# Layer norm sums on token quarters inside the convolution, a first weight transfer of its own, dummy matmuls moved, and waits by bank

## The reference, cut to what matters

```python
def conformer_conv_mixer(h, w_pw1, b_pw1, w_dw, b_dw, ln_g, ln_b, w_pw2, b_pw2):
    u = h @ w_pw1 + b_pw1
    a, gate = jnp.split(u, 2, axis=-1)
    u = a * jax.nn.sigmoid(gate)
    z = lax.conv_general_dilated(u, w_dw[:, None, :], (1,), [(CONV_WIDTH - 1, 0)], ...) + b_dw
    mu = jnp.mean(zf, axis=-1, keepdims=True)
    var = jnp.mean(jnp.square(zf - mu), axis=-1, keepdims=True)
    zf = (zf - mu) * lax.rsqrt(var + NORM_EPS) * ln_g + ln_b
    return jax.nn.silu(zf) @ w_pw2 + b_pw2
for i in range(DEPTH):
    x = x + mixer_i(rmsnorm(x, norm_mix_g[i]))          # 0: retention, 1: conformer_conv_mixer
    x = x + hierarchical_moe(rmsnorm(x, norm_ffn_g[i]))
return rmsnorm(x, final_norm_g)
```

## Time and profile before

| | |
|---|---|
| median of 3 runs | 1625.94 us (1623.56 to 1627.71) |
| profiled execution, its own time | 1625.24 us |
| its span | 1623.4 us |
| PE, DVE, ACT, POOL busy | 92%, 61%, 27%, 26% |
| mean granted clock of PE | 0.978 |
| retention and start | 0 to 441 us |
| router and experts, layer 0 | 441 to 918 us |
| norm, products, convolution | 918 to 1059 us |
| layer norm, last products | 1059 to 1129 us |
| router and experts, layer 1, final norm | 1129 to 1623 us |

### The profile page before, as it was taken

How to read it: one execution, slowest core, us unless ns; L and a number is a source line. 1 busy time by engine, 2 the same in 40 slices (tenths; PEclk the granted TensorE clock), 3 DMA queues, 4 the chain that set the end, 5 groups by cost and what they waited for, 6 DMA issues and landing times.

```text
span 1623.4 us, 45311 instructions
## 1 busy us (share of the span) xinstructions
PE 1495.5 (92%) x18938; PEld 982.5 (61%) x18939; DVE 989.1 (61%) x1662; ACT 446.2 (27%) x731; POOL 423.7 (26%) x371
## 2 busy tenths in 40 slices
PE   7999999999989999998789899979999988889996
PEld 5868778688645555554445588747555555445553
DVE  4222022220378888776566889952788877668877
ACT  5242422322432222221112422154222212112222
POOL 3434334244101212121111255523021211112121
PEclk9999999999999999999999999999999999999998
DMA  9212212122299999999999620116399999999996
GB/s 377 85 64 71 93 53 104 52 104 104 87 377 428 429 428 428 429 428 428 429 429 426 277 100 20 41 57 266 118 417 430 428 429 429 428 428 430 428 428 271
DMA packets 33849, 457.60 MB, mean 282 GB/s; under 512 B 3840, under 2 KB 3968, under 8 KB 6400
## 3 DMA queue, kind: packets, MB, share of 16 engines
q1 hardware_dynamic: 33648, 456.57, 67.4%
q10 hardware_dynamic: 144, 0.18, 0.0%
HBM read 454.64 MB, written 2.10 MB: 281 GB/s over the span
## 4 chain that ended last, share of the span: by engine, by line
PE 66%; DMA 21%; DVE 10%; issue 1%; ACT 1%; SPq 0%; POOL 0%; DVEq 0%; ACTq 0%
PE ps L803 15%; PE ps L697 9%; PE ps L699 9%; PE ps L698 9%; DMA area_b<-w_gu 9%; PE ps L820 8%; PE ps L739 7%; PE ps L786 5%; DMA ring<-w_down 5%; DMA ring<-w_gu 4%; DVE area_c L1321 4%; DMA hT<-w_down 3%; PE ps L888 2%; DVE ring L1321 2%; PE ps L880 1%
## 5 line engine op out<-in xcount | busy, mean ns | idle before, releaser
L1159 DVE TENSOR_TENSOR x<-x,ps 128x1024 f32<-128x1024 f32 x384 | 450.9, 1216 | 90.7 <-PE ps L786 90.7
L456 POOL TENSOR_SCALAR slot_tok<-trig,slot_now 128x512 fp32r<-128x512 f32 x94 | 147.0, 1563 | 710.7 <-PE ps L786 710.7
L425 POOL TENSOR_TENSOR w_lo<-ring,w_hi 128x512 fp32r<-128x512 f32 x176 | 236.8, 1348 | 359.4 <-ACT w_hi L475 359.2
L803 PE MATMUL ps<-ring,hgT 128*32 128x256 f32 x4160 | 259.5, 391 | 48.4 <-DMA ring<-w_gu 28.6
L803 PEld LDWEIGHTS ps<-ring,hgT 128*32 128x32 f32 x4160 | 131.1, 111 | 145.0 <-issue 41.1
L475 ACT CAST w_hi<-ring 128x512 fp32r<-128x512 f32 x176 | 108.9, 623 | 346.8 <-PE ps L699 346.3
L739 PE MATMUL ps<-area_a,block_rows 128*32 128x256 f32 x3072 | 187.7, 386 | 0.6 <-DVE block_rows L1120 0.6
L549 ACT ACTIVATE y_hi<-ps,slots 128x256 fp32r<-128x256 f32 x94 | 44.5, 474 | 396.7 <-PE ps L820 396.7
L739 PEld LDWEIGHTS ps<-area_a,block_rows 128*32 128x32 f32 x3072 | 102.3, 113 | 72.1 <-issue 9.5
L820 PE MATMUL ps<-ring,aT_e 128*32 128x256 f32 x2080 | 125.7, 382 | 3.6 <-DMA ring<-w_down 3.6
L697 PE MATMUL ps<-w_hi,hT_hi 128*128 128x512 f32 x320 | 125.0, 391 | 2.9 <-DVE hT_lo L1351 2.9
(11 more groups left out here) (216 smaller groups left out, 1941.5 us busy)
## 6 DMA issues: line engine op xcount, KB each, us to landing
ring<-w_gu SPq DMA_DIRECT2D x88, 2048.0 KB, 28.1
ring<-w_down SPq DMA_DIRECT2D x44, 2048.0 KB, 29.0
area_c<-w_gu SPq DMA_DIRECT2D x20, 2048.0 KB, 29.3
area_b<-w_gu SPq DMA_DIRECT2D x20, 2048.0 KB, 31.8
hT<-w_down SPq DMA_DIRECT2D x20, 2048.0 KB, 32.4
ring<-w_pw SPq DMA_DIRECT2D x6, 2048.0 KB, 10.8
ring<-w_qk SPq DMA_DIRECT2D x4, 2048.0 KB, 8.4
ring<-w_v SPq DMA_DIRECT2D x4, 2048.0 KB, 8.7
```

Of the source, the lines that this page charges most:

```text
L425: nc.gpsimd.tensor_tensor(w_lo[:, place, :], ring[:, s, at:at + 512], w_hi[:, place, :].bitcast(F32), ALU.subtract).then_inc(lo_ready, 1)
L456: nc.gpsimd.tensor_scalar(slot_tok[:, :], tok_number, slot_now[:, 0:1], None, ALU.is_equal).then_inc(tok_hot[l], 1)
L803: last = nc.tensor.matmul(ps[32 * g:32 * g + 32, 2, 0:256], hgT[:, n * (KT // 2) + k, :], gate_up[n][:, k, :, g * P:(g + 1) * P], start=(n ...
L1159: return V.tensor_tensor(x[:, i, :].rearrange("p (g c) -> p g c", g=4), x[:, i, :].rearrange("p (g c) -> p g c", g=4), ps[:, bank:bank + 4 ...
```

## The change

- **Start.** The first two weight tiles come in a DMA of their own (0.5 MB). ACT loads a table before it waits, and casts the first tiles between the norm tiles. PE runs three dummies, and `x_added` rises by 4 after half of `norm_lo`.
- **Waits by bank.** In the first product and the first product of the convolution, PE waits at bank m for `hT_lo` of tile m, no longer for four tiles at once. The two dummies and waits ahead of the latter are gone.
- **Experts.** `know_rows` for the next block stands at the head of a block instead of at the end of the one before; that after the last block is gone. Two dummies stand between the last two puts, and one instead of two after `combined` reaches 2. ACT casts only two tiles ahead of the norm.
- **Layer norm.** POOL's sum is gone. Inside the taps of m = 1, PE sums tiles 0 to 3 (`sum_channels`, four 32-column groups), and minus that sum by 512 is added as `shift` to all 8 tiles: by DVE to tiles 0 to 3 between taps, by 16 more diagonal matmuls to tiles 4 to 7. Sums of `z` and of its squares go by `sum_quarters`: four column groups, each with 128 tokens, so that all later statistics are 128x128 instead of 128x512. The variance is the mean of squares less the squared mean. `spread_quarters` puts mean and scale back on all partitions. DVE then has per tile a subtraction (`centre`), a scale that reads PSUM, and `hT_lo`.

The diff's core:

```diff
-            load_slot(0, w_qk[0])
+            sp.dma_start(ring[:, 0, 0:1024], w_qk[0, :, 0:1024]).then_inc(first_loaded, 16)
+            sp.dma_start(ring[:, 0, 1024:SLOT], w_qk[0, :, 1024:SLOT]).then_inc(slot_loaded[0], 16)
...
-                        if n == pw1_tiles + NWT:
-                            pool.wait_ge(z_ready, 2)
-                            nc.gpsimd.tensor_tensor(z_sum, z[:, 0, :], z[:, 1, :], ALU.add).then_inc(z_summed, 1)
...
+            act.wait_ge(pad_zero, 1)
+            nc.scalar.activation(small[:, 40:41], small[:, 0:1], ACT.Copy, scale=small[:, 1:2])
             act.wait_ge(par_loaded, 16)
-            norm_hi(0, 0, G_MIX, range(0, KT // 2))
+            norm_hi(0, 0, G_MIX, range(0, 2))
...
-                act.wait_ge(slot_loaded[0], 16 * h + 16)
-                split(0, 0, NWT // 2)
                 if h == 0:
-                    norm_hi(0, 0, G_MIX, range(KT // 2, KT))
-                split(0, NWT // 2, NWT)
+                    act.wait_ge(first_loaded, 16)
+                    split(0, 0, 1)
+                    norm_hi(0, 0, G_MIX, range(2, 3))
+                    split(0, 1, 2)
+                    norm_hi(0, 0, G_MIX, range(3, KT))
+                    act.wait_ge(slot_loaded[0], 16)
+                    split(0, 2, NWT)
+                else:
+                    act.wait_ge(slot_loaded[0], 16 * h + 16)
+                    split(0, 0, NWT)
...
-            split_conv(0, NWT)
+            split_conv(0, 2)
             nc.scalar.activation(small[:, 40:41], small[:, 0:1], ACT.Sqrt)
             norm_roots(1, lambda i: act.wait_ge(combined, i + 1))
-            norm_hi(2, 1, G_MIX + KT)
+            norm_hi(2, 1, G_MIX + KT, range(0, KT // 2))
+            split_conv(2, NWT)
+            norm_hi(2, 1, G_MIX + KT, range(KT // 2, KT))
...
+            act.wait_ge(half_mm, 1)
+            nc.scalar.copy(sums, ps[:, 0, :]).then_inc(half_ready, 1)
+            act.wait_ge(shift_mm, 1)
+            nc.scalar.activation(shift, ps[:, 1, :], ACT.Copy, scale=-2.0 / (BLK * D)).then_inc(shift_ready, 1)
+            for c in range(4):
+                act.wait_ge(shifted, c + 1)
                 nc.scalar.activation(z_squares[:, c, :], z[:, c, :], ACT.Square).then_inc(squared, 1)
-            act.wait_ge(var_mm, 1)
-            nc.scalar.activation(ln_root, ps[:, 3, :], ACT.Sqrt, bias=eps, scale=1.0 / D).then_inc(lnroot_ready, 1)
...
+            act.wait_ge(var_ready, 1)
+            nc.scalar.activation(ln_root, ln_var, ACT.Sqrt, bias=eps).then_inc(lnroot_ready, 1)
+            act.wait_ge(mean_mm, 1)
+            nc.scalar.activation(mean.rearrange("p (g s) -> p g s", g=4), ps[:, 4:8, 0:P], ACT.Copy,
+                                 scale=1.0 / BLK).then_inc(mean_ready, 1)
...
-                        pe.wait_ge(hTlo_ready, split[0] + max(k + 1, split[1]))
+                        pe.wait_ge(hTlo_ready, split[0] + k + 1)
...
+                        if split is not None and k == tiles[0] and 0 < m < split[1]:
+                            pe.wait_ge(hTlo_ready, split[0] + m + 1)
...
                 put_rows(0, 0, first_mm[l])
+                stay_awake(4, 2)
                 put_rows(1, 4, second_mm[l])
...
-            pe.wait_ge(hThi_ready, 1)
             pe.wait_ge(hTlo_ready, 1)
-            stay_awake(0, 2)
+            stay_awake(0, 3)
...
-            stay_awake(0, 2)
+            stay_awake(0, 1)
             pe.wait_ge(combined, NT)
             turn_norm(2)
-            pe.wait_ge(hThi_ready, KT + 1)
-            pe.wait_ge(hTlo_ready, KT + 1)
-            stay_awake(0, 2)
...
+            def sum_quarters(bank, tiles, channels, begin, end):
+                for c in channels:
+                    for g in range(4):
+                        last = nc.tensor.matmul(ps[32 * g:32 * g + 32, bank, 0:P], ones[:, 0:BLK],
+                                                tiles[:, c, g * P:(g + 1) * P], start=begin and c == channels[0],
+                                                stop=end and c == channels[-1], tile_position=(0, 32 * g))
+                return last
+            def spread_quarters(at, part):
+                for g in range(4):
+                    rows = slice(32 * g, 32 * g + 32)
+                    last = nc.tensor.matmul(ps[:, 4 + g, at:at + P], ones[rows, :], part[rows, :], start=True,
+                                            stop=True, tile_position=(32 * g, 0))
+                return last
...
+                    if m == 1 and n == 5:
+                        pe.wait_ge(z_ready, 4)
+                        sum_channels(0, z, 0, True, True).then_inc(half_mm, 1)
+                    if m == 1 and n == 8:
+                        pe.wait_ge(half_ready, 1)
+                        nc.tensor.matmul(ps[:, 1, :], ones, sums, start=True, stop=True).then_inc(shift_mm, 1)
...
+                if m == 1:
+                    pe.wait_ge(shift_ready, 1)
+                    for c in range(4):
+                        for r in range(4):
+                            rows, cols = square(r, r)
+                            nc.tensor.matmul(ps[square(r, c)[1], 4 * m + r, :], const[rows, C_EYE:C_EYE + BLK],
+                                             shift[rows, :], start=False, stop=False, tile_position=(32 * r, 32 * c))
+                    pe.wait_ge(squared, 4)
+                    sum_quarters(0, z, range(0, 4), True, False)
+                    sum_quarters(2, z_squares, range(0, 4), True, False)
...
-            parts = ((z_sum, z_summed, 3), (z[:, 4, :], z_ready, 5), (z[:, 6, :], zv_ready, 1),
-                     (z[:, 5, :], z_ready, 6), (z[:, 7, :], zv_ready, 2))
-            for n, (part, ready, count) in enumerate(parts):
-                pe.wait_ge(ready, count)
-                last = nc.tensor.matmul(ps[:, 2, :], ones, part, start=(n == 0), stop=(n == len(parts) - 1))
-            last.then_inc(mean_mm, 1)
-            for c in range(KT):
-                pe.wait_ge(squared, c + 1)
-                last = nc.tensor.matmul(ps[:, 3, :], ones, z_squares[:, c, :], start=(c == 0), stop=(c == KT - 1))
-            last.then_inc(var_mm, 1)
+            pe.wait_ge(z_ready, 6)
+            pe.wait_ge(zv_ready, 2)
+            sum_quarters(0, z, range(4, KT), False, True).then_inc(sums_mm, 1)
+            pe.wait_ge(squared, 6)
+            pe.wait_ge(squared_v, 2)
+            sum_quarters(2, z_squares, range(4, KT), False, True).then_inc(sums_mm, 1)
+            pe.wait_ge(mean_known, 1)
+            spread_quarters(0, ln_mean).then_inc(mean_mm, 1)
+            stay_awake(1, 1)
+            pe.wait_ge(mean_ready, 1)
+            pe.wait_ge(scale_known, 1)
+            spread_quarters(P, ln_scale).then_inc(scale_mm, 1)
             pe.wait_ge(u_ready, KT)
-            stay_awake(4, 5)
+            stay_awake(1, 2)
...
-                know_rows(l, 1)
...
                 with dve.Fori(0, total) as t:
+                    know_rows(l, t + 1)
                     dve.wait_ge(first_mm[l], t + 1)
...
-                    know_rows(l, t + 2)
...
-            norm_lo(0, 0, G_MIX)
-            V.sem_inc(x_added, 8)
+            norm_lo(0, 0, G_MIX, range(0, KT // 2))
+            V.sem_inc(x_added, 4)
+            norm_lo(0, 0, G_MIX, range(KT // 2, KT))
+            V.sem_inc(x_added, 4)
...
+                        if m == 1 and pair == 1 and k == 8:
+                            dve.wait_ge(shift_ready, 1)
+                            for c in range(4):
+                                V.tensor_tensor(z[:, c, :], z[:, c, :], shift, ALU.add).then_inc(shifted, 1)
...
-            dve.wait_ge(mean_mm, 1)
-            for c in range(KT):
-                V.scalar_tensor_tensor(out=z[:, c, :], in0=ps[:, 2, :], scalar=-1.0 / D, in1=z[:, c, :],
-                                       op0=ALU.mult, op1=ALU.add).then_inc(centred, 1)
+            for c in (6, 7):
+                dve.wait_ge(zv_ready, c - 5)
+                V.tensor_tensor(z_squares[:, c, :], z[:, c, :], z[:, c, :], ALU.mult).then_inc(squared_v, 1)
+            dve.wait_ge(sums_mm, 1)
+            V.tensor_scalar(ln_mean, ps[:, 0, 0:P], 1.0 / D, None, ALU.mult).then_inc(mean_known, 1)
+            dve.wait_ge(mean_known, 1)
+            link.done(V.tensor_tensor(ln_var, ln_mean, ln_mean, ALU.mult))
+            dve.wait_ge(sums_mm, 2)
+            V.scalar_tensor_tensor(out=ln_var, in0=ps[:, 2, 0:P], scalar=1.0 / D, in1=ln_var, op0=ALU.mult,
+                                   op1=ALU.subtract).then_inc(var_ready, 1)
+            def centre(c):
+                V.tensor_tensor(z[:, c, :], z[:, c, :], mean, ALU.subtract).then_inc(centred, 1)
+            def scale_z(c):
+                dve.wait_ge(centred, c + 1)
+                V.scalar_tensor_tensor(out=z[:, c, :].rearrange("p (g s) -> p g s", g=4), in0=ps[:, 4:8, P:2 * P],
+                                       scalar=1.0 / BLK, in1=z[:, c, :].rearrange("p (g s) -> p g s", g=4),
```

(12 more changed lines are left out.)

47 lines of the change are left out of this document (28 added, 19 removed).

## The result

The changed kernel takes **1608.12 us** (median of 4 runs, 1605.48 to 1611.25), the kernel before beside it 1624.97: a ratio of 0.9895 (95% interval 0.9881 to 0.9909), 17 us less. The forecast was 1608.3. The profiled execution took 1609.26 us, its span is 1607.4 (before 1623.4): -16.0. In a later comparison the same kernel took 1610.80 beside 1623.80, a ratio of 0.9912 (0.9896 to 0.9928); over all nine runs its median is 1610.3. So the gain is 13 to 17 us.

The account below looks back on a forecast made before the run. The prediction took layer 1's weight stream to bound the kernel, started by the phases ahead of it, so gains there shift the end. Terms summed to -17.6 from 1625.24, giving 1607.6, median 0.7 above: 1608.3 us; range 1602.5 to 1617.

Parts of the forecast that it names:

- A: Kernel start: first product at 14.5 instead of 18.28, plus clock regained; -5.0 us, between -3.0 and -5.9.
- B: Layer 0's last block to the convolution's first product: earlier adds, transposes and product; -4.5 us, between -2.2 and -4.9.
- D: Layer norm: shorter statistics path to the first Silu, less slower work behind it; -11.5 us, between -9 and -13.
- ACT drains at about 10.3: Start: with the table load under the transfer of x, ACT begins draining at about 10.3 us, 0.6 a tile.
- The term of -1.2 for the clock: Start: one PE gap of 0.8 us replaces two of 2.3 and 3.1, regaining most lost clock; -1.2 us.
- rival 1: PE's clock stays low where work is sparse, at start, layer 0's end and layer norm; 1613.8 us, chance 0.22.
- C: Convolution taps: added DVE and PE work makes PE end later; +3.2 us, between +2.6 and +4.7.
- The path of the statistics: Layer norm, from the taps' end to the first Silu: 23.0 us becomes 8.5; -14.5 us.
- the tail: Behind the first Silu: DVE's three operations a tile cost 0.6 us more for five tiles; +3.0 us.
- E: Kernel end: dummies make the third add wait, +0.2 us; inside the blocks the know_rows move changes 0.
- 2, the gain ends at the stream: Layer 1's refills paced by loads under way, not PE, so later gains are lost; up to 1624 us, chance 0.05.
- 3, the block's head: One-hot at the block's head lengthens all 94 expert blocks; slower, 1655 us at 1.5 us a block, chance 0.04.

Follow-up runs that it names:

- u_mid: Changed kernel without dummies between the last puts, and with the old casts, waits and two dummies (placed later) ahead of the convolution's first product: 1614.3 us.
- u_norm: Kernel before plus every part of the change except the layer norm, its shift and the sums among the taps: 1619.3 us, ratio 0.9967 to the kernel before.
- e_puts: Changed kernel without the dummies between the last puts, in both layers: 1610.2 us.
- u_rows: Changed kernel with know_rows back at a block's end, as in the kernel before: 1612.2 us.
- e_slow: Changed kernel with 14 one-column memsets on DVE ahead of know_rows at each block's head: 1611.3 us against 1610.8 in the same comparison.

## Why the prediction held

The time came within 0.2 us of the forecast, which is luck in part: over all nine runs it is 2 us off, and by the profile A and B fell short by 0.9 and 2.0 while D gave 2.1 more than forecast. The stages of no term moved as well (+0.8 to the put, -1.6 to the refill, +1.6 behind it) and nearly cancel. A slip of the working: the terms' ends add up to -21.0 and -9.3, so 1604.9 and 1616.6, and not to -20.5 and -8.3; B's own figures, 928.3 for 932.93, give -4.6. The measured time lies well inside either pair of ends. The terms:

- **A**, forecast -5.0, profile -4.1, on average -2.9. The step that failed is "ACT drains at about 10.3". The table load is off the path, but in all twelve profiles with the new start PE releases ACT later than at the old 10.24: ACT's first drain starts at 10.63 to 11.92. `x` lands no later (the last of its four transfers takes 6.9 to 7.4 us, with the old start 6.9 and 7.0). PE's transposes of `x` take 5.2 to 6.7 us, against 5.0 and 5.1, since they run longer at the slow pace of 0.213 us: they speed up at 9.3 to 12.0 us and not at 8.7, and the later they do, the later ACT starts. So the forecast took PE's pace in the transposes for granted. Two profiles of the old start are too few to tell whether the new start delays the clock or these two were early by chance; the parts of the start were not tried apart. The term of -1.2 for the clock failed too: the dip at 18 goes, but others come in retention.
- **B**, forecast -4.5, profile -2.5, mean of the seven profiles with that middle 12.2 for 15.5, so -3.3; -4.2 where the clock stays up. The steps were right (1.7 for the one-hot, measured 1.66); what remained is rival 1's mechanism, a clock of 0.50 after 2.3 us without work, in four executions of these seven. The other three had the same 2.3 us and kept 1.00, so the idle time alone does not decide it. The waits by bank, which I had not priced apart, are worth 1.9.
- **C**, forecast +3.2, measured +3.4 to +3.5 (u_mid +3.8) where the sums are unaltered. PE's new pieces come to about 5.6 us, less its slack of 2.16. I had the quarter matmuls too dear (1.2, measured 0.9 to 1.0) and the rest, above all the 16 diagonal ones, a little too cheap.
- **D**, forecast -11.5, profile -13.6. The path of the statistics was forecast at -14.5 and gave -15.4; the tail was forecast at +3.0 and was +1.7. I let five tiles pay 0.6 each, but ACT's first weight cast behind the Silu is only 1.3 late for PE, since PE starts the product at its own pace and reaches that tile later. Against u_norm D is -16.8, since in u_norm a stretch of low clock fell into it.
- **E**, forecast +0.2, measured +0.3: with the dummies 14.5 us from the first of the last two puts to the end, without them 14.2 (e_puts). Inside the blocks 0, as forecast.

**Rivals.** 1, the clock in sparse work: seen in B, not in D, and in A as a later fast pace at the start and as dips elsewhere; it was no case of its own but a spread over all of them. By the Trainium skill ("TensorE: Matmul & The Clock Gate", section "Part 1: The HAM clock gate") activity releases the throttle. The transposes at full clock behind the third dummy agree with that, in two executions; the dips of retention, with PE busy for 6 of 8 us, are not explained by it here. 2, the gain ends at the stream: refuted by u_norm. 3, the block's head: refuted by u_rows; by e_slow even a head 0.45 us longer costs nothing that shows.

## What to carry over

When a weight stream starts behind a chain of phases, price each phase from its own first row to its last, and check experiments on the same stages: four runs could not tell a 1.6 us edit that all three profiles with it showed to 0.1 us. If an engine is late, look at whether its input landed late or its own instructions ran longer: at the start it was the second. A statistic over channels that is cut into column groups makes the matmuls, the root and the reciprocal of every hand-over short, so move what need not be late (first halves, squares) under work that runs anyway, but not ahead of the matmuls that end it. Fill an idle PE right up to the next work: with 2.3 us idle the clock fell in half of the executions, with 0.6 in neither of two.

## What I had not expected

- PE's clock dips also while PE is busy: 0.79 over 8 us, up to 1.7 us each, one to three times in 450 us of retention, and more often when its first product started before 14.7. Two executions of one program differ in this (one dip and two), and different programs whose transposes sped up at the same moment have dips at the same places.
- With the new start PE's transposes of `x` release ACT 0.4 to 1.7 us later, though the four transfers of `x` are issued first, at the same time, and land at the same time.
- After the load of ACT's table at 1.15 the next activation starts at 2.45, 1.30 later, as in the earlier trace rows. The Trainium skill's further drain of 1.38 us ("ScalarE: Activation LUTs", section "What ACT_TABLE_LOAD costs") shows in neither.
- DVE's small operations took 1.25 and 1.23 us in u_rows where POOL worked beside it, and 0.29 and 0.17 in a block without it.
